# Empty matmuls at five more kinds of waits in a two-model transformer kernel

## The reference

```
def _latent_mixer(h, mem, cos, sin, p):
    proj = h @ p['w_in']
    k, v, kg, vg, gf, gb = _mem_parts(proj[..., :MEM_COLS], p)     # k is RMS-normed by head
    q, qg, r, glu, gates = _rest_parts(proj[..., MEM_COLS:], p)    # q too
    k_ctx, v_ctx, s_f, s_b = mem
    k_all = jnp.concatenate([_apply_rope(k, cos, sin), k_ctx], axis=2)
    v_all = jnp.concatenate([v, v_ctx], axis=2)
    o_att = _attend_blocks(_apply_rope(q, cos, sin), k_all, v_all)
    o_gla, _, _ = _gla_bidir(qg, kg, vg, gf, gb, s_f, s_b)
    return _merge(o_att, o_gla, r, glu, gates, p)

def _merge(o_att, o_gla, r, glu, gates, p):
    y_att = o_att... @ p['w_att_o']
    y_gla = (_rmsnorm(o_gla, p['gla_norm'])... * jax.nn.silu(r)) @ p['w_gla_o']
    y_conv = _conv_module(glu, p)          # 31-tap depthwise convolution, layernorm, silu, @ w_conv_o
    g_att, g_gla, g_conv = jnp.split(jax.nn.sigmoid(gates), N_BRANCH, axis=-1)
    return (g_att * y_att + g_gla * y_gla + g_conv * y_conv) @ p['w_out']
```

## Time and profile before

| | us |
|---|---|
| median of three runs | 2973.17 |
| lowest, highest | 2970.26, 2974.44 |
| the profiled execution | 2982.4 |
| its span in the trace | 2980.6 |
| TensorE busy | 2756.8 (92%) |
| VectorE busy | 2121.5 (71%) |
| ScalarE busy | 1526.0 (51%) |
| mean granted clock of TensorE | 0.958 |

### The profile page before, as it was taken

How to read it: one execution, slowest core, us unless ns; L and a number is a source line. 1 busy time by engine, 2 the same in 40 slices (tenths; PEclk the granted TensorE clock), 3 DMA queues, 4 the chain that set the end, 5 groups by cost and what they waited for, 6 DMA issues and landing times.

```text
span 2980.6 us, 59183 instructions
## 1 busy us (share of the span) xinstructions
PE 2756.8 (92%) x23752; PEld 2599.9 (87%) x23752; DVE 2121.5 (71%) x3683; ACT 1526.0 (51%) x3209; POOL 0.2 (0%) x4
## 2 busy tenths in 40 slices
PE   7989889999989899899989898899999899998998
PEld 6988789999988779799979887798998689996998
DVE  4987768788788777666658798877666665665655
ACT  4655345555665355454555553455445545555554
POOL 0000000000000000000000000000000000000000
PEclk8999899999999899999989898999999899998999
DMA  8554445455554334355425433344553135541454
GB/s 292 156 185 133 132 133 163 143 177 188 158 183 139 119 128 142 114 170 184 142 92 163 150 120 103 104 142 154 185 189 121 64 120 178 185 144 40 157 184 155
DMA packets 120473, 441.94 MB, mean 148 GB/s; under 512 B 13296, under 2 KB 15472, under 8 KB 118816
## 3 DMA queue, kind: packets, MB, share of 16 engines
q1 hardware_dynamic: 108416, 392.93, 40.8%
q10 hardware_dynamic: 11808, 45.42, 4.6%
HBM read 437.25 MB, written 1.05 MB: 147 GB/s over the span
## 4 chain that ended last, share of the span: by engine, by line
PE 68%; DVE 20%; ACT 6%; DMA 3%; issue 2%; SPq 0%; ACTq 0%; DVEq 0%
PE lin L466 17%; PE lin L467 17%; PE lin L468 17%; DVE arena L1831 5%; DVE w_lo L1681 4%; PE aux L593 2%; DMA w_raw<-in_stream 2%; ACT w_hi L1073 2%; DVE rstd L1706 2%; PE lin L479 1%; DMA a_raw<-in_ada 1%; PE lin L482 1%; PE lin L483 1%; PE aux L584 1%; PE aux L661 1%
## 5 line engine op out<-in xcount | busy, mean ns | idle before, releaser
L1681 DVE TENSOR_TENSOR w_lo<-w_raw,w_hi 128x1024 fp32r<-128x1024 f32 x722 | 876.2, 1221 | 351.6 <-ACT w_hi L1073 345.4
L466 PE MATMUL lin<-h_hi,w_hi 128*128 128x256 f32 x3456 | 1000.9, 290 | 5.3 <-ACT arena L1332 3.0
L467 PE MATMUL lin<-h_lo,w_hi 128*128 128x256 f32 x3456 | 987.6, 286 | 0.0
L468 PE MATMUL lin<-h_hi,w_lo 128*128 128x256 f32 x3456 | 987.1, 286 | 0.0
L1073 ACT ACTIVATE w_hi<-w_raw 128x512 fp32r<-128x512 f32 x1446 | 828.8, 623 | 280.1 <-DMA w_raw<-in_stream 185.4
L466 PEld LDWEIGHTS lin<-h_hi,w_hi 128*128 128x128 f32 x3456 | 673.6, 195 | 19.3 <-issue 8.1
L467 PEld LDWEIGHTS lin<-h_lo,w_hi 128*128 128x128 f32 x3456 | 673.6, 195 | 0.4
L468 PEld LDWEIGHTS lin<-h_hi,w_lo 128*128 128x128 f32 x3456 | 673.0, 195 | 0.0
L466 PE MATMUL lin<-s_hi,w_hi 128*128 128x256 f32 x1520 | 449.2, 295 | 22.1 <-DVE s_lo L1767 15.5
L467 PE MATMUL lin<-s_lo,w_hi 128*128 128x256 f32 x1520 | 438.3, 288 | 0.0
L468 PE MATMUL lin<-s_hi,w_lo 128*128 128x256 f32 x1520 | 437.9, 288 | 0.0
(11 more groups left out here) (277 smaller groups left out, 3679.8 us busy)
## 6 DMA issues: line engine op xcount, KB each, us to landing
w_raw<-in_stream SPq DMA_DIRECT2D x723, 512.0 KB, 3.5
a_raw<-in_ada ACTq DMA_DIRECT2D x80, 512.0 KB, 3.5
arena<-in_first SPq DMA_DIRECT2D x6, 1024.0 KB, 14.0
X<-in_tokens SPq DMA_DIRECT2D x2, 1024.0 KB, 13.1
s_f<-in_first SPq DMA_DIRECT2D x2, 1024.0 KB, 17.7
arena<-in_const ACTq DMA_DIRECT2D x1, 1856.0 KB, 11.2
arena<-in_small ACTq DMA_DIRECT2D x1, 1536.0 KB, 14.3
out<-arena SPq DMA_DIRECT2D x1, 1024.0 KB, 3.9
```

The costliest lines, as they stand in the source:

```text
L466: used(pe.matmul(o, whi, hi[:, k, :], start=k == 0, stop=False), first)
L467: pe.matmul(o, whi, lo[:, k, :], start=False, stop=False)
L468: mm = pe.matmul(o, wlo, hi[:, k, :], start=False, stop=k == kcs - 1)
L1681: dve.tensor_tensor(w_lo[:, m % SLOTS, :], w_raw[:, m % RAW, :], w_hi[:, m % SLOTS, :].bitcast(F32), ALU.subtract).then_inc(sems["lo_ready ...
```

## The change

A new function `hold(k)` issues k matmuls of 128x256 fp32 on constants (`mean1024`, and the first 256 columns of `const1`) into the bank of `lin` that comes next. It does not take the bank: the next `bank()` gets the same one and starts its sum anew. Before them it waits until that bank has been copied out, for the count `lin_done - 3`. Nobody reads the result. It stands at five kinds of places:

- `gla`, step 0: six, ahead of the wait for the first level (three passes)
- `heads_normed`: three, ahead of the wait for `row_ready` (four passes)
- `heads_normed` in latent passes: five, ahead of the wait for the rotated heads (two passes)
- `attention` of the first block: five at j = 2, between the scores of item 2 and the transposes of item 0 (three passes)
- the merge: five ahead of the first dense product, and ahead of them a wait until four chunks of `s` are split (three passes)

That is 15 places with 3 x 6 + 4 x 3 + 2 x 5 + 3 x 5 + 3 x 5 = 70 matmuls. Other engines' programs stay as they are. The second block calls `attention` with empty fills and gets none.

```diff
+            def hold(k):
+
+                if n.at("lin_done") >= 4:
+                    pe.wait_ge(sems["lin_evac"], n.at("lin_done") - 3)
+                for _ in range(k):
+                    pe.matmul(lin[at.bank][:, 0:S], c1("mean1024"), const1[:, 0:S], start=True, stop=True)
+
             def head_rows(chunks):
...
                     if j < len(items):
                         scores(j)
+                    if j == 2 and fill[0]:
+                        hold(5)
                     if 2 <= j < len(items) + 2:
                         transposes(j - 2)
...
                     pair = [aux[2 * (j % 2)], aux[2 * (j % 2) + 1]]
+                    if j == 0:
+                        hold(6)
                     if j < STEPS - 1:
                         pe.wait_ge(sems["lev_ready"], at.up("lev_ready"))
...
             def heads_normed(heads, s, beside, run):
 
+                hold(3)
                 pe.wait_ge(sems["row_ready"], at.up("row_ready"))
...
                 if s == LAT:
                     rotate(heads, len(heads) - 1, q0, r0)
                     n.up("qk_ready", len(heads))
+                    hold(5)
                     pe.wait_ge(sems["qk_ready"], n.at("qk_ready"))
...
                     ready = "s_ready", n.at("s_ready")
                     n.up("s_ready", KC)
+                    pe.wait_ge(sems["s_ready"], ready[1] + 4)
+                    hold(5)
                     for c in range(KC):
                         dense(s_hi, s_lo, ready if c == 0 else None)
```

## The result

The changed kernel takes 2956.4 us in the median of five runs (2950.0 to 2959.0); the one before took 2970.3 us beside it. The ratio is 0.9946, 95% interval 0.9931 to 0.996. A second series gave 2952.9 against 2970.9 us, ratio 0.9939 (0.9924 to 0.9954). So by the ratios it is 16 to 18 us faster (14 and 18 by the medians), where the prediction said 7 us, 2966, with a range of 2953 to 2979. The direction was right. The first measurement lies in the range, the second at its lower end; the gain that was forecast is less than half of the measured one.

The account below looks back on a forecast made before the run. The prediction took TensorE, busy 92% of the span with a dipping clock, as the bound; 2.5 + 0.5 + 0.5 + 1.0 + 1.0 + 1.5 = 7.0 us off the 2973.2 us median gave 2966 us, range 2953 to 2979.

Parts of the forecast that it names:

- The price of an empty matmul: At all 15 places: 0.216 us for one at the full clock, 15.1 us of TensorE for all 70.
- the prediction's own classes: TensorE waits by length: 2.8 us up, 16 of 16 fell; 1.9-2.7, 16 of 17; 1.6-1.9, 6 of 10; 1.4-1.6, 2 of 12.
- case C: At the 15 places: waits up to 2.6 us with solid work ahead keep the clock; 20 us gained, 2953; chance 0.11.
- What the falls would do with waits of that length: At the 15 places: with 1.8 to 3.1 us of wait left, some falls are avoided, for 7.0 us in sum.
- the prediction's last sign: At 27 waits left alone: falls lost or gained by the time shift, 1.5 to 3 us each, would make it wrong.
- Case B: At the 15 places: falls come by wait length alone, so little changes; about 3 us gained, 2970; chance 0.27.
- The share that is kept: Behind avoided falls: all of the gain at level 0, first pass (2.5 us); 0.2 to 0.4 at rotation and first probabilities.
- The bound of 30 us: At the 15 places: the most the change can win, 70.17 us of busy TensorE at the lower clock x 0.43.
- 0.43 us lost for each busy microsecond at the low clock: On TensorE: dense matmuls start 0.21 us apart at the lower clock, 0.12 at the full one; 0.43 us lost.
- The cover of the holds: At 14 of 15 places: waits of 2.0 to 4.4 us hide the empty matmuls; up to 15.1 us cost if missing.
- The one place without a wait: First probabilities, first pass: five empty matmuls move transposes 0.8 us, hidden by a 1.31 us wait for an ada partial; cost 0.
- Case D: At merge, rotation, first probabilities: falls come later, with the low clock on dense work; +8 us, 2981; chance 0.16.

Follow-up runs that it names:

- half-size kernel: The changed kernel with 3 empty matmuls at level 0, 1 at head rows, 2 at the other kinds: 2970.4 us against 2970.3 before, ratio 0.9996.
- the wait alone: The changed kernel without any empty matmul, keeping only the merge's new wait for the fourth chunk: ratio 0.9999 to the kernel before.
- the halves: The changed kernel with matmuls only at level 0, head rows, merge (2963.5 us), or only at rotation, first probabilities (2965.7 us): each 0.9985 to before.

## Why the prediction came out as it did

**The price of an empty matmul** failed, by a factor of two. The prediction read ten matmuls out of the row, and took 0.216 us for one. That row is `keep_clock(IDLE // 2)`, five matmuls: an fp32 matmul makes two records, each of 128x256. One costs 0.43 us. (The dense products read tiles that the kernel declares float32r; each of them is one record, though the rows say f32 for both.) The counts would have told: the calls of `keep_clock` ask for 100 matmuls in all, and the group of L600 has 200 records; after the change there are 140 more, for 70 matmuls. In the group view of the kernel before:

```profile
L600 PE MATMUL aux<-const 128*128 128x256 f32 x200 | 47.8, 394 | 0.0
```

So all waits were cut by twice what was reckoned, to 0.9 to 1.5 us (0.4 at the merge) instead of 1.8 to 3.1. By the prediction's own classes (1.4 to 1.6 us: 2 of 12 fell) nearly all falls then go. The measured 16 to 18 us are near the 20 us of its case C, but not for that case's reason, that waits of up to 2.6 us keep the clock: waits of that length were not left. The step that failed is this one term, and the half-size kernel is the check on it: it has the waits that were reckoned with, and no gain of it can be told. That the time lies in the range is owed to the range reaching up to case C, which had a chance of 0.11, and not to the sum.

**What the falls would do with waits of that length** was too hopeful. For just those waits the prediction gave 7 us; measured are 1.2 us (-1.5 to 3.9). The prediction read from one profile, place by place, how long TensorE had been idle when the clock fell. Of its eight readings at level 0, rotation and first probabilities, five came out in the half kernel's profile (kept: level 0 of the first pass, rotation of the second, probabilities of the fourth; fell: level 0 and rotation of the fourth). Three did not: the probabilities of the first pass fell, and level 0 and the probabilities of the second held. That moment is not a property of the place: the 3.44 us of level 0 brought the clock down in the one profile and not in the other, with nothing changed there. Two executions of the full change have 27 low stretches each ahead of the last matmul, and 21 of them are at the same place. So the prediction's last sign, falls gained or lost at places left alone, comes between runs of one kernel too and tells nothing. Case B of the prediction, the count by length alone, said 3 us, which the half kernel's interval holds. The rule of the Trainium skill that the prediction named ("TensorE: Matmul & The Clock Gate", "Why this matters for your kernels": no idle gaps over about 3 us) would have had these waits, 1.7 to 2.8 us, harmless; the clock fell at 10 of the 15, so it does not hold here. Two errors thus worked against each other: matmuls half as long as they are, and too much hope in half-filled waits.

**The share that is kept** failed as well. By the shares of the chain it was 0.2 to 0.4 in the attention and all of it at level 0. The table of distances has what was kept, full change against the wait alone. Rotation of the second pass: 5.75 us of work at the lower clock, priced 2.5 and given 1.0, gave 2.3. First probabilities of the second pass: given 0, gave 1.5. Head rows of the second pass: given 1.0, gave 2.1. First probabilities of the fourth: given 0.5, gave nothing. Over all runs 0.24 to 0.30 of 0.39 us is kept, some two thirds to three quarters. That DVE stood in the chain of the attention with its taps did not mean that TensorE's time is free there. Why it is free in one pass and not in the other was not tested.

**The bound of 30 us.** Taken whole, the low stretches at the 15 places of before are 92 us long, with TensorE busy in 80 of them; the earlier trace rows has 77.90 and 70.17. The bound would be 34 us. The last line of the same view over the whole stretches:

```profile
sum 92.16, PE 79.54; mean PE 5.30
```

**What held.** 0.43 us lost for each busy microsecond at the low clock: the rotation of the second pass gave 2.3 of the 2.5 us that this makes. The cover of the holds: with the empty matmuls counted in, the waits at head rows, rotation and first probabilities of the second pass are 2.42, 3.40 and 3.67 us in all 14 traces, with empty matmuls there or without, and the one at level 0 of the first pass is 3.44 us. So neither they nor `hold`'s own wait for the bank cost anything there. The one place without a wait, the first probabilities of the first pass, is covered by the wait for the ada partial, though the matmuls there took 2.16 us instead of 1.08:

```profile
340.24 2.32 PE L614 MATMUL lin<-const 128*128 128x256 f32 x10
342.40 0.60 PE L656 MATMUL aux<-const,arena 128*128 128x128 f32 x4
342.84 0.28 PE L506 MATMUL lin<-const,ada_part 128*128 128x2 f32 x2
343.40 0.43 PE L517 MATMUL lin<-a_raw,cvec 128*32 128x128 f32 x8 [0.28 <-DMA a_raw<-in_ada]
```

The scores began at 339.38, so the ada unit came 4.02 us behind them; before it was 347.63 - 343.48 = 4.15 us. The wait of 1.31 us is gone and nothing came later. The new wait of the merge shows no cost (0.9999, 0.9989 to 1.0008).

**Case D**, falls that only come later, did not carry the result. At the merge of the first pass it did happen: the low stretch of before began at 467.7, 2.6 us into the wait; after, it begins at 462.8, between the seventh chunk and the last, and lies mostly on the dense work behind. Leaving the merge's matmuls out is slower still in the median (0.9958), though not beyond the uncertainty.

**Open.** The parts give less alone than together: 0.9985 and 0.9985 for the halves, 0.9943 for the whole, and the same tendency in the runs with one kind left out. The intervals of the halves just reach what adding up would need. In the mean clock of the runs the halves come closer to it: 0.0065 and 0.0031 more than before, together 0.0096, against 0.0127 for the full change in the second series. And at the places of the table each gain is there alone as it is together. So what is missing must lie in other stretches, such as the level stage of the fourth pass; what decides there was not settled.

## What to carry to other kernels

Where TensorE's clock falls in short waits, fill the waits with matmuls that nobody reads, and fill them until about 1 us is left: half filled they gave nothing. Pick waits that are long in the trace and behind which the clock is low. Judge by time over several runs: the mean granted clock is a guide, here 14 to 18 us for each 0.01, but it rose by 0.0035 in a kernel that gained no time. Do not build on the moment at which the clock fell in one profile. Before using a row's count as a number of matmuls, set it against the code: an fp32 matmul counts twice, one on float32r tiles once.

## What the runs showed of the hardware

- An fp32 matmul of 128x256 is two records and 0.43 us at the full clock (2.75 us for six, 2.32 for five in a row).
- With waits of 1.7 to 2.8 us left behind 0.4 to 1.3 us of empty matmuls at 14 of the 15 places, the clock still fell at 10 of the 15; with 0.4 to 1.5 us left it fell at 2 or 3, one of them between two waits.
- A wait of 3.44 us at the same place, in programs that are the same up to there, brought the clock down in one execution and not in another.
- 6.8 us less at the lower clock made two stretches of the program 2.0 to 2.7 us shorter in every kernel; 3.4 us less made a third 1.3 to 1.5 us shorter and a fourth not at all.
- Empty matmuls showed no cost in their cover even when they left only 0.3 to 0.6 us of it (0.9932 against 0.9939).
